# A two-block transformer layer in float32: the first modulation product on TensorE, and kv and qa as one job by quarters of K

## The reference, cut to what matters

```python
mod = (c @ w_ada[l] + b_ada[l])[:, None, :]            # c: 2048 values, w_ada: 2048 x 12288
shift1, scale1, gate1, shift2, scale2, gate2 = jnp.split(mod, N_MOD, axis=-1)
h = rmsnorm(x, g_pre_mix[l]) * (1.0 + scale1) + shift1
proj = h @ w_in[l]
q_a, k_a, v_a, q_h, f_h, i_h, g_h, gate_a, gate_h = jnp.split(proj, splits, axis=-1)
```

## Time and profile before

| | |
|---|---|
| median of 3 runs | 2618.37 us (2618.26 to 2620.07) |
| the profiled execution | 2619.33 us |
| its span | 2617.0 us |
| PE busy | 2543.8 us, 97% of the span |
| DVE busy | 1832.7 us, 70% |
| ACT busy | 1304.1 us, 50% |
| DMA from HBM | 547.14 MB, mean 210 GB/s |
| stage loads of `w_ada` | 64 of 512 KB, 9.7 us from issue to landing |

### The profile page before, as it was taken

How to read it: one execution, slowest core, us unless ns; L and a number is a source line. 1 busy time by engine, 2 the same in 40 slices (tenths; PEclk the granted TensorE clock), 3 DMA queues, 4 the chain that set the end, 5 groups by cost and what they waited for, 6 DMA issues and landing times.

```text
span 2617.0 us, 42035 instructions
## 1 busy us (share of the span) xinstructions
PE 2543.8 (97%) x15000; PEld 2232.1 (85%) x15000; DVE 1832.7 (70%) x2265; ACT 1304.1 (50%) x1693; POOL 28.1 (1%) x32
## 2 busy tenths in 40 slices
PE   4899999999999999999999999999999999999999
PEld 4888888888787888888888877888888888888888
DVE  6789998777788555677555566566677774477774
ACT  1345566566445444444444445455555554455543
POOL 0000000000000000000000000030000000000000
PEclk9699999999999999999999999999999999999999
DMA  9899984554594666798666555644655556555565
GB/s 371 302 341 313 313 294 152 167 161 153 184 315 136 193 192 186 237 307 270 189 191 189 190 169 176 186 146 150 188 177 186 188 189 206 186 184 192 186 197 164
DMA packets 493560, 550.70 MB, mean 210 GB/s; under 512 B 18856, under 2 KB 450992, under 8 KB 493456
## 3 DMA queue, kind: packets, MB, share of 16 engines
q1 hardware_dynamic: 492032, 544.20, 63.9%
q0 software_dynamic: 1424, 5.13, 0.7%
HBM read 547.14 MB, written 2.11 MB: 210 GB/s over the span
## 4 chain that ended last, share of the span: by engine, by line
PE 79%; DVE 11%; issue 5%; ACT 3%; DMA 1%; SPq 1%; DVEq 0%; ACTq 0%
PE psg L1886 74%; PE pss L1886 4%; DVE w_lo L1211 2%; DVE gate_acc_mix L1198 2%; ACT w_hi L670 2%; DVE first_acc L1282 1%; SPq L540 1%; DMA stage<-in_w_ada 1%; DVE proj L1170 0%; DMA raw<-in_w_in 0%; DVE Pq L1419 0%; DVE decay L1421 0%; DVE decay L1408 0%; DVE decay L1407 0%; DVE masked L1433 0%
## 5 line engine op out<-in xcount | busy, mean ns | idle before, releaser
L1886 PE MATMUL psg<-X,w_hi 128*128 128x512 f32 x4512 | 1579.8, 394 | 10.2 <-DVE proj L1170 5.8
L1211 DVE TENSOR_TENSOR w_lo<-raw,w_hi 128x1024 fp32r<-128x1024 f32 x832 | 1008.2, 1228 | 602.9 <-ACT w_hi L670 593.4
L670 ACT ACTIVATE w_hi<-raw 128x1024 fp32r<-128x1024 f32 x832 | 867.7, 1057 | 804.9 <-PE psg L1886 754.6
L1886 PE MATMUL psg<-X,w_lo 128*128 128x256 f32 x4512 | 1250.5, 282 | 0.0
L1886 PEld LDWEIGHTS psg<-X,w_hi 128*128 128x128 f32 x4512 | 843.0, 189 | 187.2 <-issue 11.8
L1886 PEld LDWEIGHTS psg<-X,w_lo 128*128 128x128 f32 x4512 | 855.4, 190 | 12.5 <-issue 1.4
L1886 PE MATMUL psg<-hid,w_hi 128*128 128x512 f32 x1664 | 575.8, 392 | 0.2 <-issue 0.2
L1886 PE MATMUL psg<-hid,w_lo 128*128 128x256 f32 x1664 | 458.5, 280 | 0.0
L1886 PEld LDWEIGHTS psg<-hid,w_hi 128*128 128x128 f32 x1664 | 309.8, 188 | 66.3 <-issue 0.6
L1886 PEld LDWEIGHTS psg<-hid,w_lo 128*128 128x128 f32 x1664 | 312.6, 188 | 3.3
L664 ACT ACTIVATE half<-psg 128x512 f32<-128x512 f32 x204 | 118.4, 581 | 3.5 <-PE psg L1886 3.3
(11 more groups left out here) (306 smaller groups left out, 1536.9 us busy)
## 6 DMA issues: line engine op xcount, KB each, us to landing
raw<-in_w_in SPq DMA_DIRECT2D x212, 512.0 KB, 4.2
raw<-in_w_ffn_in SPq DMA_DIRECT2D x176, 512.0 KB, 4.1
raw<-in_w_up SPq DMA_DIRECT2D x176, 512.0 KB, 4.9
raw<-in_w_ffn_out SPq DMA_DIRECT2D x88, 512.0 KB, 4.5
raw<-in_w_down SPq DMA_DIRECT2D x88, 512.0 KB, 3.4
gate_w_mix<-in_w_ada SPq DMA_DIRECT2D x160, 256.0 KB, 5.3
stage<-in_w_ada SPq DMA_DIRECT2D x64, 512.0 KB, 9.7
raw<-in_w_out SPq DMA_DIRECT2D x64, 512.0 KB, 4.3
```

Source lines behind the costliest of these rows:

```text
L670: nc.scalar.activation(w_hi[:, half_slot(j, p), :, :], raw[:, slot_of(j, p), :, :], ACT.Copy).then_inc(hi_ready, 1)
L1211: nc.vector.tensor_tensor(w_lo[:, hs, :, :], raw[:, slot_of(j, p), :, :], w_hi[:, hs, :, :].bitcast(F32), ALU.subtract).then_inc(raw_used, 1)
L1886: return nc.tensor.matmul(out_, l, r_, start=start, stop=stop)
```

## The change

1. The 4096 first columns of `w_ada` are formed as 8 blocks of 512 columns, in the order 4, 0, 5, 1, 6, 2, 7, 3 (scale and shift of one quarter of K after the other). A load is two K-tiles of a block, 512 KB, in a ring of 10 slots; there are still 64. **DVE has no part in these products any more.** For every two loads PE does four float32 matmuls (`first_rows`), each with a 128x32 stationary operand (c of one K-tile in column 0, zeros in the others) and the 512 columns of one K-tile as the moving one, into PSUM partitions 0, 32, 64 and 96 of one bank. ACT copies the bank (`rows_out`), PE sums it over partitions (the new `first_sum`, 4 products), and DVE adds the bias.
2. kv and qa are one job, qkv: 20 groups of one chunk each, five (k and v, then the four of q) for each quarter of K. The first five groups store their sum in `proj`; the others add to it, which takes DVE one more add on `half`. Between its chunks stand the rows and sums of the blocks that are still missing, and SP's queue interleaves its loads with the stage loads by two lists, `FIRST_LOADS` and `NEXT_LOADS`.
3. The two gate blocks that stood beside qa become "slow" ones: one beside m1, one beside gh, each 4 steps a turn. The slow block of gh starts at p = 0 of its first turn.
4. The swap and turn of k and v move to the end of qkv, and the tables (`bounds`) into its first chunks.

The core of the diff:

```diff
-ADA_CB = 1024
-STAGES = 12
+ADA_CB = 512
+STAGES = 10
-FIRST_BLOCKS = (2, 0, 3, 1)
+FIRST_BLOCKS = (4, 0, 5, 1, 6, 2, 7, 3)
...
-            Job("kv", 1, [wide(w_in, 0, DT, KA * P)]),
-            Job("qa", 2, [wide(w_in, 0, DT, 0, 2 * CW), wide(w_in, 0, DT, CW, 2 * CW)], spread(8)),
+            Job("qkv", 1, [wide(w_in, 4 * q, 4, c0) for q in range(4) for c0 in (KA * P, 0, CW, 2 * CW, 3 * CW)]),
...
+        FIRST_LOADS = (17, 19, 21, 23)
+        NEXT_LOADS = (29, 33, 35, 37, 39, 41, 49, 51, 53, 55, 57, 60, 62)
+        SLOW = {"m1": (0, (4, 7, 9, 11)), "gh": (1, (0, 2, 4, 6))}
...
+            for n in range(8 * ADA_FIRST):
+                b, k, s = FIRST_BLOCKS[n // 8], 2 * (n % 8), n % STAGES
+                if n >= STAGES:
+                    sp.wait_ge(stage_used, (n - STAGES) // 2 + 1)
+                sp.dma_start(stage[s][:, :, :], ada_v[:, k:k + 2, b * ADA_CB:(b + 1) * ADA_CB]).then_inc(staged[s], 16)
...
+                if n in NEXT_LOADS:
+                    p = NEXT_LOADS.index(n)
+                    load(jobs[0], 0, p, w_src(*ahead(jobs[0], 0, p, True)))
...
+            def load_slow(j, i, kk):
...
+                if is_first(i) and kk == 0:
+                    sp.wait_ge(ada_mm, j.m0 + j.iters * j.blocks)
+                    sp.wait_ge(gate_used, J["hg"].a0 + J["hg"].iters * len(J["hg"].ada))
...
+            def rows_out(b):
+                act.wait_ge(stage_used, 4 * b + 4)
...
+                nc.scalar.activation(rows[:, :], pss[:, 2 + b % 2, :], ACT.Copy).then_inc(row_out, 1)
...
+                def side(i, p, final):
+                    if p < 15 and p % 5 == 0:
+                        rows_out(2 * (p // 5) + 2)
+                    if p < 15 and p % 5 == 4:
+                        rows_out(2 * (p // 5) + 3)
...
+                if j.name == "qkv" and g >= 5:
+                    here(nc.vector.tensor_tensor(dst, dst, half[:, b // 2, :, :], ALU.add))
+                    nc.vector.tensor_tensor(dst, psg[:, b:b + 2, 0:CW], dst, ALU.add).then_inc(ps_free, 1)
+                    return
...
+            def slow_step(j, i, kk):
...
+                dve.wait_ge(slow_in[kk % 2], 16 * (8 * n + kk // 2 + 1) + i * 32)
+                if is_first(i) and kk == 0:
+                    dve.wait_ge(ada_mm, j.m0 + j.iters * j.blocks)
...
+                        if p == 2 and is_first(i) and j.prev is not None and j.prev.slow:
+                            slow_sum(j.prev)
...
+            def first_rows(b, *groups):
+                for t in groups:
...
+                    for a in range(4):
+                        n = 8 * b + 2 * t + a // 2
+                        ins = mm(pss[32 * a:32 * a + 32, 2 + b % 2, :], c_rows[:, 4 * t + a, :],
+                                 stage[n % STAGES][:, a % 2, :], t == 0, t == 3)
+                    ins.then_inc(stage_used, 1)
...
+                def side(i, p):
+                    b = 2 * (p // 5) + 2
+                    if p < 15 and p % 5 == 0:
+                        first_rows(b, 3)
+                    if p < 15 and p % 5 == 1:
+                        first_rows(b + 1, 0)
+                        first_sum(b)
+                    if p < 15 and p % 5 in (2, 3):
+                        first_rows(b + 1, p % 5 - 1)
+                    if p < 15 and p % 5 == 4:
+                        first_rows(b + 1, 3)
+                        if p < 14:
+                            first_rows(b + 2, 0)
+                        first_sum(b + 1)
+                        if p < 14:
+                            first_rows(b + 2, 1, 2)
```

More of the change, by code:

```diff
@@ L580, in job_turn @@
                             load_gate(j, i, k)
-            for j in live:
-                all_turns(sp, j, job_turn, bool(j.ada))
+                    if j.slow and p in SLOW[j.name][1]:
+                        load_slow(j, i, SLOW[j.name][1].index(p))
+            for j in live[1:]:
+                all_turns(sp, j, job_turn, bool(j.ada or j.slow))
             if runs("dn2b"):
@@ L786, in side @@
                         ins.then_inc(S1["vo"], 1)
-                    if p == 5:
-                        act.wait_ge(S1["dup"], 2)
-                        for b in range(4):
-                            g = b // 2
-                            ins = nc.scalar.activation(kd4[:, b, :], pss[:, 1, g * S:(g + 1) * S], ACT.Copy)
-                        ins.then_inc(S1["dupo"], 1)
-                job(J["qa"], side=side)
+                job(J["qkv"], after, side)
+                act.wait_ge(S1["dup"], 2)
+                for b in range(4):
+                    g = b // 2
+                    ins = nc.scalar.activation(kd4[:, b, :], pss[:, 1, g * S:(g + 1) * S], ACT.Copy)
+                ins.then_inc(S1["dupo"], 1)
             def one(a):
@@ L1231, in turn @@
                                 gate_step(j, i, k)
+                        if j.slow and p in SLOW[j.name][1]:
+                            slow_step(j, i, SLOW[j.name][1].index(p))
+                        if p == 3 and is_first(i) and j.prev is not None and j.prev.slow:
+                            gate_result(j.prev.m0 + j.prev.iters * j.prev.blocks)
                         if side:
@@ L1296, in first_scale @@
[L1296 to L1305 removed]
+            here(nc.vector.memset(c_rows[:, :, :], 0.0))
@@ L1390, in side @@
                         nc.vector.tensor_tensor(kr[:, :], kr[:, :], ang[:, :], ALU.add).then_inc(S1["kr"], 1)
-                job(J["qa"], lambda i, g: proj[:, ds(4 * i + 2 * g, 2), :], None, side)
+                job(J["qkv"], lambda i, g: proj[:, KA:KA + 2, :] if g % 5 == 0 else proj[:, 2 * (g % 5) - 2:2 * (g % 5), :], after, side)
             cum = decay[:, 6, :]
@@ new lines, in first_sum @@
+            def first_sum(b):
+                pe.wait_ge(row_out, b + 1)
+                if b >= 2:
+                    pe.wait_ge(ada_out, b - 1)
+                for t in range(4):
+                    o = 8 * b + 2 * t
+                    ins = mm(pss[:, (b + 1) % 2, o:o + 2], rows[:, t * P:(t + 1) * P], ones[:, 0:2])
+                ins.then_inc(ada_mm, 1)
+            pe.wait_ge(c_set, 1)
+            pe.wait_ge(ones_set, 2)
+            first_rows(0, 0, 1, 2)
+            norm_sum(sq1, (0,))
```

307 lines of the change are left out of this document (140 added, 167 removed).

## The result

The changed kernel takes 2628.47 us (median of 5 runs, 2627.01 to 2631.53) against 2618.38 us of the kernel before on the same chip: ratio 1.0037, 95% interval 1.0026 to 1.0048, so about 10 us slower. The forecast was "no difference that can be told", at 2618.0 us; the time lies just inside its range of 2606 to 2629 us, but the kernel is slower, not unchanged. The profiled execution took 2627.01 us, its span is 2625.2 us, 8.2 us longer than the span before. It is the fastest of the five, and the profiled one of before is 1.0 us above its median, so these two executions are 7.7 us apart (their spans 8.2), not 10.

The account below looks back on a forecast made before the run. Bound: mostly PE (79% of the chain), DMA in the first 100 us, DVE in hg. Terms -11.3 + 1.9 + 1.5 + 7.5 = -0.4 us against the profiled 2619.33 us; 2618.0 us on the median's footing, range 2606 to 2629 us.

Parts of the forecast that it names:

- no difference that can be told: Whole kernel: likeliest outcome, 2618.0 us, its own range 2613 to 2623 us, chance 0.40.
- Products in groups of four: PE in qkv: four 32-column products run side by side, 1.04 us a group; 3.44 us if one after another.
- Rival 2: PE between chunks of quarters 1 and 2: groups don't overlap, 2627 us or 2673 us; chance 0.26.
- The first stretch: Stage before hg: hg starts at 162.7 us and its DVE work earlier, a gain of 11.3 us.
- the landing of chunk 8: Loads in qkv: lands at 76.3 us by byte count; ACT's row copy for quarter 1 stands behind it.
- Chunk 13: Loads in qkv: lands at 107.8 us, held behind stage loads 54 and 55; quarter 2 follows at 114.6 us.
- Quarters 2 and 3: End of qkv: quarter 2 takes 20.6 us, then a hand-over of 6.3 us, quarter 3 from 141.5 us.
- The late load at hg's start: hg's start: 5.44 us of waiting for a load behind gate loads on SP; no such wait remains.
- The first turn of gh: Slow step 0 waits for m1's slow sum, delaying chunk 5's `w_lo` to 565.2 us: 7.5 us lost.
- The slow blocks otherwise: Behind hg: two gate sums cost 1.9 us, slow steps beside gh 1.5 us, beside m1 0.
- The clock: PE in qkv: chunks partly cold at the lower clock level; quarter 3 includes 1.5 us for this.
- The forecast's lower bound: Stage before hg: no gain if each hand-over between quarters takes 3 us more.

Follow-up runs that it names:

- Run 3: The changed kernel with a ring of 12 slots instead of 10 for the first blocks' loads; 2621.34 us, ratio 1.0005.
- run 4: The changed kernel with finished groups handled ahead of the next chunk's parts on ACT and DVE, and a ring of 12; 2614.67 us, ratio 0.9979.
- run 5: As run 4, and gh's slow block gets an accumulator of its own; 2605.62 us, ratio 0.9948.
- run 9: As run 5, with products, sum and making of the next quarter of the operand one chunk earlier; 2597.53 us, ratio 0.9917.
- run 2: The changed kernel with finished groups handled ahead of the next chunk's parts on ACT and DVE in qkv; 2614.71 us, ratio 0.9981.
- run 1: The changed kernel with an accumulator of its own for gh's slow block; 2622.83 us, ratio 1.0010.
- run 8: As run 1, with both slow blocks' loads, steps and sums left out; 2618.30 us, ratio 0.9992.

## Why the prediction was wrong

- **Products in groups of four: right.** The forecast took 1.04 us a group, with 3.44 us as the far end. A group on PE, and the first product of the chunk behind it:

```profile
54.28 1.06 PE L1914 MATMUL pss<-stage,c_rows 128*32 128x512 f32 x8
55.28 0.50 PE L1914 MATMUL psg<-X,w_hi 128*128 128x512 f32 x1
```

  It is 1.00 us from the group's start to the next one's; the first matmul behind it takes 0.50 us where one within a chunk takes 0.39. Cold (at the lower clock), a group takes 1.94 us. Rival 2 has fallen. The Trainium skill ("TensorEngine Tiling (Array Packing)", Tiling Modes, Key Properties) says that a change of tiling mode drains the engine; the trace shows no more than those 0.11 us of it, and at most 0.03 can be the change of mode, since the first matmul behind a sum over the full array takes 0.47 us as well. The estimate from the Trainium skill ("TensorE: Matmul & The Clock Gate", Part 3, Packing small matmuls), 1.08 us, was close too.
- **The first stretch: this is the step that failed.** The forecast had a gain of 11.3 us; the trace has 1.5, and other executions of the same code none. The step is the landing of chunk 8, taken from "the n-th byte count B lands at 100 - (38.4 - B)/0.41": 76.3 us, and it came at 83.7. What hangs on a landing was right: from chunk 8's `w_hi` to quarter 1 the forecast had 83.4 - 76.3 = 7.1 us, and it took 90.97 - 83.70 = 7.3. The byte count supposes queues that never wait, and the ring stood already at loads 36 and 37, from 63.8 to 71.6 us; I had looked for its gap at loads 54 and 55 only. Run 3, in which the DMA moves 387 GB/s through that gap for 319 (SP's queue still stands from 67.8 to 71.9 us), has chunk 8 at 80.85 us, so this much of the gap is worth 2.9 of the 7.4 us. Of the other 4.5 us the rate is a part: 0.41 MB per us came from loads of 1024 columns (409 GB/s from 62 to 100 us before, 3.1 KB a packet); with loads of 512 columns (1.6 KB a packet) runs 4, 5 and 9, whose DMA is full, move 394 to 399. Run 4 had moved 28.1 MB by 76.3 us, not 28.7, an estimated 1.6 us. What makes up the rest stays open.
- **Chunk 13: mostly inherited.** It came at 117.2 us, not at 107.8. Its row on ACT:

```profile
117.17 1.06 ACT L693 ACTIVATE w_hi<-raw 128x1024 fp32r<-128x1024 f32 x1 [4.71 <-DMA raw<-in_w_in]
```

  Quarter 1 had begun 7.6 us late, and a wait of 2.68 us for a bank at chunk 8 came on top. From the ring's release (110.6 us) to the landing it took 6.6 us, 6.3 in the forecast, and from there to quarter 2 7.3 us, 6.8 in the forecast. The forecast named `rows_out` behind `w_hi` but not that the half sum of every chunk stands there as well, so that each late landing delays PE's group, the group the ring, and the ring the next landing. Runs 2 to 4 show this loop: opened at either place it lets go, and opened at both it gives no more (or the DMA engines have no more to give, as said at run 4).
- **Quarters 2 and 3: right in their lengths.** Quarter 2 took 20.15 us (20.6 forecast), the last hand-over 7.4 (6.3). The last quarter took from 152.04 us to hg's chunk 0 at 172.2 us, 20.2 us (21.2). So hg began 9.5 us later than the 162.7 us of the forecast, beyond the 168 us that it had named as the sign of being wrong. The late load at hg's start is gone, as forecast: it gave 3.9 us, for 4.2.
- **The first turn of gh: right.** 7.5 us were forecast, and the removal of the wait gave 8.3 (run 1). That `w_lo` ended at 565.55 us; I had 565.2.
- **The slow blocks otherwise: 3.4 us forecast, 4.9 measured** (run 8). In gh it is 2.1 us for the forecast's 2.4, in wh 1.0 for 0.9. I gave m1 nothing, and the two traces have 1.8 us between `q_cos` and gh's heads. That is hardly above the scatter: the eight kernels with all loads and both blocks take 366.7 to 368.0 us there, the two without these blocks 365.7 and 366.1.
- **The clock.** It was granted at 0.80 from 40 to 100 us, a mix of its two levels (1.2 and 2.4 GHz), against 0.61 before, and quarter 3 began at the lower one after an idle 4.64 us: its first chunk took 4.81 us from first start to last end, where a warm one takes 3.05. That was in the forecast with 1.5 us.

Had the gain been set at zero, the same sum would have given 10.9 us of loss, and 10 were measured. The forecast's lower bound for that step was "no gain if each hand-over takes 3 us more"; the hand-overs were right within 1.1 us each, and the late landings, with the bank wait behind them, took nearly all of it.

## What to carry to other kernels

Where an engine's program at step p first prepares step p+4 and then finishes step p, every late transfer for p+4 delays p. That need not cost anything while transfers are far ahead, and here it cost the whole gain, where the transfers wait, through a ring, for p. Put what others wait for now ahead of what waits for a landing, and only then judge rings and bytes: here the order gave 13.7 us, and the larger ring nothing on top. It also steadied the kernel: the executions of run 1, which has the old order, lie 9.3 us apart, those of runs 2 and 4 only 3.3 and 3.0. And a buffer that two accumulations share across a job's border makes the second one's first step wait for the last reader of the first; a second buffer, or a later first step, is the remedy.

When forecasting a stretch in which loads and compute feed each other, don't take landings from a byte rate alone: walk the issuing queue's waits one by one, and take the rate from loads of the same shape.

## What was not expected of the hardware

Four float32 products side by side in 32-column groups of the array cost 1.00 us, little more than one full float32 product of as many columns (0.86 us). Loads whose packets are half as long (1.6 KB for 3.1) moved some 3% fewer bytes a second with the engines full (396 for 409 GB/s from 62 to 100 us, run 4 and the kernel before); no run changed this alone. And one execution of the same first part differs from another by up to 3.8 us: `q_cos` came at 182.42, 184.23, 184.30 and 186.17 us in four kernels that share the code ahead of it (but for run 8's `memset`). They did not all run on the same chip, so part of this may be the chip.
